# A two-model fp32 transformer stack on one core: rotary key rows inside the scan, logits tile by tile, and a new order of work at the start

## The reference, cut to what matters

```python
# first block, per layer (swiglu_ffn: hidden width 2816)
x = x + 0.5 * swiglu_ffn(rmsnorm(x, ffn1_norm), wi, wo)
...   # mLSTM, sliding-window attention with a relative position bias, gates, FFN, per-layer gate
# second block, per layer
h = rmsnorm_2(x, g)
uv, z, xbc, dt, c_q, c_kv, k_rope = split(h @ w_in_2)
g1 = gmlp_mixer(uv)
y  = state-space scan in chunks of 128, 6 heads of 64, over silu(conv(xbc)), dt
yg = y * silu(z)                     # the gate
g2 = rmsnorm_2(yg, in two groups of 192) * norm_g     # "root sums": 1 / sqrt(mean(yg^2))
q  = rmsnorm_2(c_q) @ w_qb           # 6 heads of 64 + 32 (rotary)
kv = rmsnorm_2(c_kv) @ w_kvb         # 6 heads: 64 of key, 64 of value
k  = [k_nope, rotary(k_rope)]        # the rotary part is shared by all heads
g3 = causal softmax(q k^T / sqrt(96)) v
x  = x + [g1, g2, g3] @ w_out_2
x  = x + squared_relu_mlp(rmsnorm_2(x, g'))
```

## Time and profile before

| | |
|---|---|
| median of 3 runs | 3460.84 us (3459.49 to 3460.96) |
| the profiled execution's own time | 3458.42 us |
| its span, first to last instruction | 3455.8 us |
| TensorE busy | 3409.1 us, 99% of the span |
| DVE, ACT, GpSimd busy | 47%, 30%, 45% |
| mean granted clock | 0.995 |
| DMA over the span | 311.25 MB, mean 90 GB/s |

### The profile page before, as it was taken

One profiled execution on the slowest core, in us unless ns is written; L12 is line 12 of the kernel. 1 busy time (PEld: TensorE's weight loads), 2 busy tenths in 40 slices (PEclk: granted clock), 3 DMA queues, 4 the chain that ended last, 5 costly groups with the idle time before them and its releaser, 6 DMA issues.

```text
span 3455.8 us, 43463 instructions
## 1 busy us (share of the span) xinstructions
PE 3409.1 (99%) x15514; PEld 2748.9 (80%) x15514; DVE 1610.7 (47%) x1956; ACT 1040.4 (30%) x1380; POOL 1546.8 (45%) x1159
## 2 busy tenths in 40 slices
PE   8999999999999999999999999999999999999998
PEld 7888876788888888887678888876788887678887
DVE  5442235654423644123665442476480726647161
ACT  3222234332222322223433222245421123632112
POOL 4444433354444544443345444442354544236442
PEclk9999999999999999999999999999999999999999
DMA  4333322233333333232223333231233323123332
GB/s 147 98 95 96 108 77 64 74 104 97 94 102 96 95 95 96 97 110 73 61 80 99 96 97 104 85 95 42 68 98 97 97 95 82 42 68 104 98 97 79
DMA packets 496141, 311.25 MB, mean 90 GB/s; under 512 B 41784, under 2 KB 454811, under 8 KB 496027
## 3 DMA queue, kind: packets, MB, share of 16 engines
q1 hardware_dynamic: 494316, 307.21, 30.3%
q10 hardware_dynamic: 1711, 2.44, 0.2%
HBM read 305.94 MB, written 3.67 MB: 90 GB/s over the span
## 4 chain that ended last, share of the span: by engine, by line
issue 38%; PE 32%; POOL 26%; DVE 1%; POOLq 0%; DVEq 0%; ACT 0%; DMA 0%; ACTq 0%
POOL wl L483 26%; PE bank L521 5%; PE bank L525 5%; PE bank L502 5%; PE bank L506 5%; PE bank L507 5%; PE bank L527 4%; PE bank L1121 1%; PE mb L1148 1%; PE bank L528 1%; PE mb L572 1%; PE mb L1060 0%; POOLq L480 0%; POOLq L478 0%; DVE sd_p L2159 0%
## 5 line engine op out<-in xcount | busy, mean ns | idle before, releaser
L483 POOL TENSOR_TENSOR wl<-raw,wh 128x512 fp32r<-128x512 f32 x1152 | 1546.0, 1364 | 1871.5 <-ACT wh L1270 1871.4
L1270 ACT ACTIVATE wh<-raw 128x1024 fp32r<-128x1024 f32 x576 | 608.2, 1057 | 1583.2 <-PE bank L502 746.8
L521 PE MATMUL bank<-xh,wh 128*128 128x512 f32 x2384 | 933.0, 391 | 0.0
L525 PE MATMUL bank<-xl,wh 128*128 128x512 f32 x2384 | 928.3, 389 | 0.0
L527 PE MATMUL bank<-xh,wl 128*128 128x512 f32 x2086 | 812.6, 390 | 0.0
L521 PEld LDWEIGHTS bank<-xh,wh 128*128 128x128 f32 x2384 | 447.8, 188 | 104.3 <-issue 11.2
L525 PEld LDWEIGHTS bank<-xl,wh 128*128 128x128 f32 x2384 | 447.9, 188 | 91.9
L502 PE MATMUL bank<-hh,wh 128*128 128x512 f32 (+1 forms) x1216 | 473.2, 389 | 0.0
L507 PE MATMUL bank<-hh,wl 128*128 128x512 f32 (+1 forms) x1216 | 473.0, 389 | 0.0
L506 PE MATMUL bank<-hl,wh 128*128 128x512 f32 (+1 forms) x1216 | 473.0, 389 | 0.0
L527 PEld LDWEIGHTS bank<-xh,wl 128*128 128x128 f32 x2086 | 391.9, 188 | 82.1
(11 more groups left out here) (382 smaller groups left out, 3130.4 us busy)
## 6 DMA issues: line engine op xcount, KB each, us to landing
raw<-in_ffn_wi_dram SPq DMA_DIRECT2D x176, 512.0 KB, 3.7
raw<-in_mlp_w_dram SPq DMA_DIRECT2D x128, 512.0 KB, 3.9
raw<-in_w_in_dram SPq DMA_DIRECT2D x102, 512.0 KB, 3.7
raw<-in_ffn_wo_dram SPq DMA_DIRECT2D x88, 512.0 KB, 3.6
raw<-in_w_out_dram SPq DMA_DIRECT2D x32, 512.0 KB, 3.8
raw<-in_w_ple_gate_dram SPq DMA_DIRECT2D x16, 512.0 KB, 3.8
raw<-in_w_a_dram SPq DMA_DIRECT2D x8, 512.0 KB, 3.3
raw<-in_w_b_dram SPq DMA_DIRECT2D x8, 512.0 KB, 3.3
```

What stands on the lines that cost most here:

```text
L483: last = gp.tensor_tensor(wl[j][:, part], raw[j % RAW_SLOTS][:, part], wh[j][:, part].bitcast(F32), ALU.subtract)
L521: first = pe.matmul(out[0:width, :], h[:, c:c + width], rh[:, k, :], start=k == 0, stop=False)
L525: pe.matmul(out[0:width, :], h[:, c:c + width], rl[:, k, :], start=False, stop=False)
L1270: act.activation(wh[n % SPLIT_SLOTS][:], raw[n % RAW_SLOTS][:], ACT.Copy).then_inc(s.hi_ready, 1)
```

## The change

At the start:
- SyncE's order stays. ACT first loads only layer 0's rows of the first gain (first_rows); all gain rows go into one zeroed tile, tables, which two full transposes turn; these run inside first_units behind its second unit, and DVE copies them out behind the first norm's inversion. The loads of the constants and of sel4 go behind the rounding of slab 2, the write of the position table behind ACT's second SiLU of the first FFN.
- TensorE transposes tiles 0 to 3 of x into mb, token tile by token tile, with the table product behind the second, and then tiles 4 to 7 into bank 0 to 3, feature tile by feature tile. DVE splits tiles 0 to 3 straight from PSUM; ACT copies them to x_sb afterwards. The square of the first half now stands ahead of slab 2's rounding.
- GpSimd also signals the first half of a split (half_split), on which the first halves of the first four units wait.

In scan and attention:
- key_rotary is cut in two: the products go into pair 0 behind the last split of the latents, the sums into pair 1 behind y_add(1). Their tiles lie elsewhere. Behind the scan weights of pair 2 stand query_scale, query 0, query 1, y_add, gate; queries 2 and 3 behind it. TensorE's order of queries and sums is as before.
- The logits use bank (MLA_BANK + c) % 4, and each of the first four waits for the tile of values that stood in its own bank.
- ACT does an Exp of one column behind the roots.

```diff
@@ gpsimd
+            gp.drain()
+            gp.memset(tables[:], 0.0).then_inc(s.consts_ready, 1)
...
-                    last.then_inc(s.split_done, 1)
+                        last.then_inc(s.split_done if half else s.half_split, 1)
@@ first_units
+                        if setup and not half:
+                            pe.wait_ge(s.half_split, u + 1)
+                            pe.wait_ge(s.setup_copied, u + 1)
+                        elif setup or not half:
+                            take_slab(B, L, n + u)
...
+                        elif setup and u == 1:
+                            tables_turned()
@@ TensorE, start
-                for j in range(KT):
-                    if t == 0 and j == KT - 1:
+                for j in range(4):
+                    if t == 0 and j == 3:
                         pe.wait_ge(s.setup_read, 1)
-                    last = turn(x_banks[j][:, t * P:(t + 1) * P], x_tok[:, t, j * P:(j + 1) * P])
...
+                    last = turn(mb[:, j, t * P:(t + 1) * P], x_tok[:, t, j * P:(j + 1) * P])
+                    if t == NT - 1:
+                        last.then_inc(s.setup_t, 1)
+                if t == 1:
+                    pe.wait_ge(s.consts_ready, 3)
+                    pe.matmul(bank[3][:, 0:TOEP], rel_wide[:].rearrange("k h r -> k (h r)"), onehot[:], start=True, stop=True)\
+                      .then_inc(s.rel_psum, 1)
+            for j in range(4, KT):
+                if j == KT - 1:
+                    pe.wait_ge(s.toep_row, 1)
+                for t in range(NT):
+                    last = turn(bank[j - 4][:, t * P:(t + 1) * P], x_tok[:, t, j * P:(j + 1) * P])
+                last.then_inc(s.setup_t, 1)
+
+            def tables_turned():
+
+                pe.wait_ge(s.setup_rows, 16 * N_ROWS)
+                pe.wait_ge(s.setup_copied, KT)
+                for l in range(2):
+                    last = turn(B5[:, l * P:(l + 1) * P], tables[:, l, :])
+                last.then_inc(s.setup_t, 1)
@@ TensorE, mla
-                pe.wait_ge(s.rot_done, at(L, 2, 2))
-                pe.wait_ge(s.tile_evacuated, tiles_out(B, L, T2_KVB + 6))
+                pe.wait_ge(s.keys_done, at(L, 1, 1))
...
+                    else:
+                        pe.wait_ge(s.tile_evacuated, tiles_out(B, L, T2_KVB + 3 + c))
+                    out = bank[(MLA_BANK + c) % TILE_BANKS]
@@ ACT, ffn
+                if L == 0 and k == 0:
+                    act.wait_ge(s.toep_row, 1)
+                    act.dma_start(scratch.rearrange("h (r e) c -> (h r) e c", e=SW_H),
+                                  toep[:, None, :].to_broadcast([P, SW_H, TOEP])).then_inc(s.toep_out, 16)
@@ ACT, start
+            act.wait_ge(s.consts_ready, 1)
+            act.activation(small[:, 0:1], ones[:, 0:1], ACT.Copy)
...
+            round_hi(Block1, None, 0)
+            copy_x(4)
+            copy_x(5)
+            round_hi(Block1, None, 1)
+            copy_x(6)
+            copy_x(7)
+            for j in range(4):
+                act.wait_ge(s.xl_ready, j + 1)
+                act.activation(x_sb[:, j, :], mb[:, j, :], ACT.Copy).then_inc(s.setup_copied, 1)
+            act.drain().then_inc(s.x_final, 1)
+            square_half(Block1, None, 0, 0)
+            round_hi(Block1, None, 2)
             act.dma_start(const[:, P:CONSTS], a["const_pack"][:, P:CONSTS]).then_inc(s.setup_const, 16)
             act.dma_start(sel4[:], a["sel4"]).then_inc(s.setup_const, 16)
@@ ACT, mla
                 act.activation(y_root[1][:], tmp[0][:], ACT.Sqrt).then_inc(s.y_rs, 1)
+                act.activation(small[:, 60:61], ones[:, 0:1], ACT.Exp)
@@ DVE, start
+            dve.wait_ge(s.rel_psum, 1)
+            dve.tensor_scalar(toep[:], bank[3][:, 0:TOEP], -1.0, None, ALU.mult).then_inc(s.toep_row, 1)
             for j in range(4):
-                dve.wait_ge(s.setup_copied, X_ORDER.index(j) + 1)
-                x_times_gain(j, g_first)
...
+                dve.wait_ge(s.setup_t, 2 + j)
+                x_times_gain(j, g_first, mb)
@@ DVE, ssd
                         latent(4).then_inc(s.c_split, 1)
+                        rotary_products(L)
                         more_in2(L, U_Z)
...
                         y_add(1)
+                        rotary_sums(L)
                         more_in2(L, U_Z + 2)
...
-                        key_rotary(L)
                         query_scale(L)
                         query(L, 0)
+                        query(L, 1)
                     y_add(i)
```

More of the change, by code:

```diff
@@ L97 @@
     norms, base_norm = 2, 8
+MLA_BANK = (Block2.base_tile + T2_KVB + 3) % TILE_BANKS
 class Last:
@@ L186, in program @@
         x_tok = at_kb("x_tok", 0, [P, NT, D])
-        rows1 = at_kb("rows1", 16, [R1, 2, P])
-        rows2 = at_kb("rows2", 17, [R2, 2, P])
-        rows3 = at_kb("rows3", 18, [KT, P])
+        tables = at_kb("tables", 16, [P, 2, P])
+        rows1, rows2, rows3 = tables[0:R1], tables[R1:R1 + R2], tables[R1 + R2:R1 + R2 + KT, 0, :]
+        first_rows = at_kb("first_rows", 17, [KT, P])
         onehot = at_kb("onehot", 19, [33, TOEP])
@@ L574, in turn @@
                 return pe.matmul(out, in_, const[0:k, C_IDENT:C_IDENT + k], start=True, stop=True)
[L578 removed]
             pe.wait_ge(s.setup_first, 2 * 16)
[L580 removed]
+            turn(B7[:, 0:KT], first_rows[:], KT).then_inc(s.setup_t, 1)
             for t in range(NT):
                 pe.wait_ge(x_landed[t], 16)
[L583 to L584 removed]
+                for j in range(4):
+                    if t == 0 and j == 3:
@@ L595, in _ @@
-            pe.wait_ge(s.consts_ready, 2)
-            pe.wait_ge(s.setup_copied, X_ORDER.index(5) + 1)
-            pe.matmul(B5[:, 0:TOEP], rel_wide[:].rearrange("k h r -> k (h r)"), onehot[:], start=True, stop=True)\
-              .then_inc(s.rel_psum, 1)
-            pe.wait_ge(s.setup_copied, 6)
+                    last = turn(mb[:, j, t * P:(t + 1) * P], x_tok[:, t, j * P:(j + 1) * P])
[5 more added lines that the diff above has]
+                      .then_inc(s.rel_psum, 1)
@@ L601, in ffn @@
             def ffn(L, k, n, t, wh_count):
-                first_units(Block1, L, n, t, k)
+                first_units(Block1, L, n, t, k, setup=L == 0 and k == 0)
                 with pe.Fori(1, FT // 2) as i:
@@ L1119, in logits @@
                         pe.wait_ge(s.ae_ready, at(L, 24, c - TILE_BANKS + 1))
-                    out = bank[c % TILE_BANKS]
+                    else:
+                        pe.wait_ge(s.tile_evacuated, tiles_out(B, L, T2_KVB + 3 + c))
+                    out = bank[(MLA_BANK + c) % TILE_BANKS]
                     pe.matmul(out[:, 0:(n + 1) * P], q_all[h][:, n * P:(n + 1) * P], k_all[:, h, 0:(n + 1) * P],
@@ L1601, in mla @@
                     w = (n + 1) * P
-                    act.activation(prob[:, c % 4, 0:w], bank[c % TILE_BANKS][:, 0:w], ACT.Exp,
+                    act.activation(prob[:, c % 4, 0:w], bank[(MLA_BANK + c) % TILE_BANKS][:, 0:w], ACT.Exp,
                                    bias=small[:, 32 + n:33 + n], scale=-1.0).then_inc(s.ae_ready, 1)
@@ L1676, in split_rows, with x_times_gain @@
                    .then_inc(s.rows_split, 1)
-            def x_times_gain(j, g):
-                x = x_sb[:, j, :]
+            def x_times_gain(j, g, source=x_sb):
+                x = source[:, j, :]
                 dve.tensor_scalar(xh[:, j, :], x, g[:, j:j + 1], None, ALU.mult)
@@ L2186, in ssd, with rotary_products @@
                 dve.tensor_tensor(conv[:, 0:3, :], proj2[:, 4:7, :], conv[:, 0:3, :], ALU.mult).then_inc(s.y_done, 1)
-            def key_rotary(L):
+            def rotary_products(L):
                 rows, again = slice(64, MLA_D), slice(MLA_D, P)
@@ L2193, in key_rotary, with rotary_sums @@
                 dve.tensor_tensor(swapped[rows, :], proj2[again, 12, :], rope[again, :], ALU.mult)
+            def rotary_sums(L):
+                rows, again = slice(64, MLA_D), slice(MLA_D, P)
                 dve.drain()
@@ L2200, in mla @@
                 B = Block2
-                for h in range(1, 4):
+                for h in range(2, 4):
                     query(L, h)
@@ L2215, in mla @@
                        .then_inc(s.tile_evacuated, 1)
-                dve.drain().then_inc(s.rot_done, 1)
+                dve.drain().then_inc(s.keys_done, 1)
                 def biggest(c):
@@ L2221, in biggest @@
                     dve.wait_ge(s.al_ready, at(L, 24, c + 1))
-                    dve.tensor_reduce(small[:, 32 + n:33 + n], bank[c % TILE_BANKS][:, 0:(n + 1) * P], AX.X, ALU.min)\
+                    dve.tensor_reduce(small[:, 32 + n:33 + n], bank[(MLA_BANK + c) % TILE_BANKS][:, 0:(n + 1) * P], AX.X, ALU.min)\
                        .then_inc(s.am_ready, 1)
```

67 lines of the change are left out of this document (22 added, 45 removed).

## The result

The changed kernel takes 3442.96 us (median of six executions, 3437.68 to 3445.91) against 3460.19 us for the kernel before beside it (3457.61 to 3461.06): ratio 0.9948, 95% interval 0.9938 to 0.9957. It is faster by 17 us, inside the range, 3.5 us above the forecast time. The profiled execution of the changed kernel took 3438.94 us with a span of 3437.2, which is 18.6 us less than the span before.

The account below looks back on a forecast made before the run. TensorE, busy 99% of the span, was taken as the bound, so only its waits or lower clock could give time back. Start 4.6 plus attention 16.7 gave 21.3 us, hence 3437.1 profiled and 3439.5 median; range 3435 to 3447.

Parts of the forecast that it names:

- The chain: Scan to latent attention: taking the rotary's 6.0 us off cuts TensorE's idle from 5.7 to 0.4 us, gaining 5.3 a layer.
- the scale keeps its 1.66: Scan's end, DVE: query scale starts at 2380.2 while a GpSimd split runs, still takes 1.66 us, ends at 2381.9.
- query 1's copy: Scan's end, DVE: now ahead of the gate, it adds a copy of 0.69 us; 1.2 us priced in altogether.
- The clock term: Sums behind the squares' wait: a 0.4 us pause leaves the clock high, gaining 2.65 us in layer 0, 2.1 in layer 1.
- The handover: Values to logits: each logits tile waits only for its own value tile, so the 0.72 us wait goes, 0.7 a layer.
- The gate and the split: Rival at the scan's end: GpSimd's split goes first, the gate waits 1.3 us per layer; +2.6 us, 3442; chance 0.20.
- The moved position table: Write of 1.5 MB, 6.6 us, behind the second SiLU: may delay slab loads within the slack; cost 0, end 4 us.
- The early Exp: ACT before the value copies: moves the 1.28 us table load off TensorE's path; worth 0, ends 0 and 0.3 us.
- The start: First units: first weight matmul at 13.9, sum of squares from 33.83 to 29.2; gain 4.6 us, ends 2 and 6.
- The bound of 30.3: Start's sums: upper end of 28.9 to 30.3, adding 1.4 us if each of the three adds meets a split.
- the lower clock costs the same few microseconds in both kernels and hides behind the splits: Start: the lower clock makes no difference between the kernels, so no term was given to it.
- a pause of 1.99 us leaves the clock alone: Start: idle 1.99 us ahead of the sum at 33.83 was followed by clock 1.00, so 0.4 us should be harmless.

Follow-up runs that it names:

- start alone: The kernel before with only the start's half of the change, attention as before: 3455.39 us, ratio 0.9981 to the kernel before.
- filled-wait kernel: The kernel before with six added, unread TensorE products ahead of its wait for the squares in both layers: 3457.98 us, ratio 0.9992.
- no early Exp: The changed kernel without the one-column Exp that loads ScalarE's table early: 3437.99 us, ratio 0.9940 to the kernel before.
- filled split wait: The changed kernel with two added, unread TensorE products in the wait for x's split behind attention: 3437.60 us, ratio 0.9937 to the kernel before.

## Why the prediction was right, and by how much not

**The chain was read right.** The 5.72 us wait went. Forecast was a rest of 0.4 us; TensorE doesn't wait at all, since the scale took 0.68 and not 1.66 us. The mis-sized term is this scale: the step "the scale keeps its 1.66" took the split to be running when the scale comes. It was, from 2376.33, 0.15 us ahead of the scale, but here GpSimd was the slower one (3.21 us for two halves, against 2.55 for the undisturbed pair at 2369.13). What I priced at about 0.6 us a layer, query 1's copy, costs nothing for the same reason: with the scale 1 us shorter the copies end at 2378.53 and y_add waits for TensorE's scan products until 2379.09 in any case. From the scan products to the sums it is now 6.62 us instead of 12.40, and DVE's and ACT's chain is through 0.09 us ahead of TensorE's own units. A longer chain would show again.

**The clock term was right**: 2.65 and 2.1 forecast, 2.54 and 1.93 with the wait filled. **The handover** was 0.7, measured 0.87. **Attention together**: 16.7 forecast, 9.20 + 8.58 = 17.8 between the marks. Of the 1.1 us more, 1.0 is the wait's, with two times 5.8 us for two times 5.3.

**The gate and the split**, a rival with 0.20, didn't come: the gate took 1.76 us, the split started 0.77 us behind it. **The moved position table** cost nothing: TensorE has no wait from 44 to 90 us. **The early Exp** is worth 0, as priced.

**The start: the mis-sized term.** Forecast 4.6, measured 3.3 in the sum's start (33.83 to 30.52), and 3.3 in U where the clock holds, 1.7 where it falls behind the new wait. The first matmul was 0.2 us late, and that close by luck: the forecast had the half split as the last to come and the transposes through at about 11.8, where the last transpose begins at 14.0. The sum came 1.3 us late. The mis-sized term is the splits of two more tiles of x, which ended 1.7 us late: forecast from 22.8 to 26.1, as 1.6 us a tile, where a tile is two operations and three of the four met a GpSimd split (1.31, 1.63, 1.51 and 0.75, from 22.53 to 27.80, 5.3 us). The three adds gave 0.4 us back: they took their free 2.75, where the forecast of 29.2 had allowed 3.1. The bound of 30.3 was nearly the result. The step that failed outright is "the lower clock costs the same few microseconds in both kernels and hides behind the splits". In the kernel before, the clock was low from ahead of its first weight matmul (17.61) to 22 us:

```profile
16.00:22.00 6.00, 5.23 (x12) 3.43 (x11) 5.80 (x7) 2.54 (x4) 4.61 (x4) 0.50 0.33 92
```

In the changed kernel it was 1.00 from the first weight matmul to the sum and fell only behind the sum's wait. There the second half of the four units follows without a wait, so what the lower clock costs is lost.

**What the sum left out.** Take each kernel's own S to G, U without a fall behind the sum's wait, and for the other pieces the smallest value of all traces. Then the kernel before takes 45.72 + 2332.61 + 32.64 + 562.54 + 32.03 + 448.09 = 3453.6 us of span, the changed one 42.38 + 2332.61 + 23.44 + 562.54 + 23.43 + 448.09 = 3432.5 (U from the start alone, whose code there is the same; it also has the old attention, whose two S to G add to 64.62 us there and to 64.67 before). The difference is 21.1 us against 21.3 forecast; that two errors of opposite sign, 1.3 less at the start and 1.1 more in attention, cancelled is luck. By the medians only 17.2 us were gained. In the profiled pair clock falls add 2.2 us to before and 4.7 to after; that the whole 3.9 us between 21.1 and 17.2 are such falls is taken over from there, not shown. That a pause of 1.99 us leaves the clock alone rested on a single execution; the filled-wait kernel had the fall behind that very pause. A trace shows what one execution did, so a clock that held once is half an argument.

**The page's rule on PSUM sources** (the Trainium skill, VectorE: DVE Perf Modes, "Why PSUM operands drop a tier"): seen for one step of the two, and outweighed. Undisturbed, the rounding takes 0.47 from SBUF and 0.75 from PSUM, the way the rule has it; the other step, xl, takes 0.75 from either. Beside GpSimd the SBUF steps take up to 1.6 and the PSUM ones still 0.75. The measurement decided for PSUM here: the sum is ready 1.7 us earlier, by the steps and by the copies that they need not wait for.

## What to carry to other kernels

Look first at what stands on the one chain behind which TensorE waits, and move off it whatever has its inputs earlier: four small operations moved into idle time were worth 8 us a layer, more than their own duration, because most of them were contended there and because the wait slowed the matmuls behind it. Price such an operation by its row at that place, beside what the other engines do there, not by its undisturbed row, and check at which of the two engines the loss falls: the scale's went to GpSimd. And measure between marks that both kernels share: with the changed attention S to G repeats to 0.04 us in nine traces, while whole executions of one kernel spread over 8.

## What had not been expected of the hardware

- The granted clock fell to 0.50 at places where TensorE did little: behind waits of 1.99 to 6.32 us, and among the small products at the scan's start, where it counts as busy but for a wait of 0.6 us; in some executions and not in others of the same kernel. Such falls lengthened the piece with a scan's start by 1.3 to 5 us (2332.61 to 2337.7, 562.54 to 567.04) and the start by 1.5, and cost nothing behind the split wait.
- The start wait of 2.4 us was followed by a fall in five profiles (U at 43.83 to 44.15) and by none in three (start alone, no early Exp, filled split wait: 42.38 to 42.52), though all eight run the same start. What decides between them no run here shows.
- DVE and GpSimd slowed each other where both worked from SBUF: DVE's 0.68 became 1.64 to 1.81, GpSimd's two halves 2.55 became up to 3.38, and which of them pays differs from place to place. DVE's steps from PSUM kept their 0.75 beside a split, and GpSimd's four halves beside them took 5.01, as undisturbed ones do.
